# Indexed attention of the first block: index dots ahead of the query products, VectorE's list in a new order, a later fourth query product, an earlier start of the output product

## The reference, cut to what matters

```
q, c, qi, ki, wi = split(h @ w_in)            # 1024, 128, 8x64, 64, 8 columns
c = rms_norm(c, kv_norm_g)
dots  = relu(einsum('bqhd,bsd->bqhs', qi, ki))            # 8 index heads
score = einsum('bqh,bqhs->bqs', wi, dots), causal
idx   = top_k(score, 64)                                  # per query
logits = (q @ w_uk * scale) . c[idx] + rel_bias, causal   # 16 heads
o = softmax(logits) . c[idx] @ w_uv
x = x + o @ w_o ;  x = x + relu(norm(x) @ w_up)**2 @ w_down
```

## Time and profile before

| | us |
|---|---|
| median of 3 runs (range) | 885.27 (882.36 to 885.95) |
| the profiled execution: its time | 883.13 |
| its span | 881.0 |
| TensorE busy | 858.1 (97%) |
| VectorE busy | 686.0 (78%) |
| ScalarE busy | 474.8 (54%) |
| GpSimd busy | 137.3 (16%) |

### The profile page before, as it was taken

How to read it: one execution, slowest core, us unless ns; L and a number is a source line. 1 busy time by engine, 2 the same in 40 slices (tenths; PEclk the granted TensorE clock), 3 DMA queues, 4 the chain that set the end, 5 groups by cost and what they waited for, 6 DMA issues and landing times.

```text
span 881.0 us, 17947 instructions
## 1 busy us (share of the span) xinstructions
PE 858.1 (97%) x7016; PEld 818.4 (93%) x7016; DVE 686.0 (78%) x1074; ACT 474.8 (54%) x698; POOL 137.3 (16%) x154
## 2 busy tenths in 40 slices
PE   6999999999999987899999999999999999999998
PEld 5998999999999985599999999999889999999998
DVE  4897789898876698667666677678658998997884
ACT  7783365555444346656655444354357647645742
POOL 6230100014311000000000122232204213013000
PEclk9999999999999997999999999999999999999999
DMA  9755767779998432046655666656536554454652
GB/s 348 256 209 188 269 219 250 241 241 281 264 256 214 151 108 84 2 144 197 206 192 194 196 197 196 195 190 191 178 130 194 150 176 155 145 190 147 198 185 96
DMA packets 46960, 167.86 MB, mean 191 GB/s; under 512 B 5776, under 2 KB 5920, under 8 KB 46640
## 3 DMA queue, kind: packets, MB, share of 16 engines
q1 hardware_dynamic: 40896, 146.82, 50.6%
q0 software_dynamic: 5856, 20.00, 8.3%
q10 hardware_dynamic: 144, 0.15, 0.1%
HBM read 165.50 MB, written 1.44 MB: 189 GB/s over the span
## 4 chain that ended last, share of the span: by engine, by line
PE 90%; DVE 6%; ACT 2%; issue 1%; DMA 1%; POOL 0%; DVEq 0%; SPq 0%; ACTq 0%
PE bank L551 25%; PE bank L547 25%; PE bank L552 25%; PE bank L618 5%; PE bank L636 2%; PE bank L781 1%; DVE wlo L1329 1%; PE bank L876 1%; PE bank L886 1%; PE bank L835 1%; PE bank L837 1%; PE bank L836 1%; DVE score L1631 1%; DVE lt L1680 1%; DMA plain<-plain_w 1%
## 5 line engine op out<-in xcount | busy, mean ns | idle before, releaser
L1329 DVE TENSOR_TENSOR wlo<-raw,whi 128x1024 fp32r<-128x1024 f32 x260 | 320.5, 1265 | 91.7 <-ACT whi L971 91.4
L551 PE MATMUL bank<-xl,whi 128*128 128x256 f32 x1328 | 369.6, 278 | 0.0
L552 PE MATMUL bank<-xh,wlo 128*128 128x256 f32 x1328 | 368.4, 277 | 0.0
L547 PE MATMUL bank<-xh,whi 128*128 128x256 f32 x1310 | 367.4, 280 | 0.2 <-DVE wlo L1329 0.2
L971 ACT ACTIVATE whi<-raw 128x1024 fp32r<-128x1024 f32 x260 | 265.6, 1053 | 144.7 <-PE bank L552 129.3
L547 PEld LDWEIGHTS bank<-xh,whi 128*128 128x128 f32 x1310 | 245.8, 188 | 9.2 <-issue 7.4
L551 PEld LDWEIGHTS bank<-xl,whi 128*128 128x128 f32 x1328 | 249.4, 188 | 0.3
L552 PEld LDWEIGHTS bank<-xh,wlo 128*128 128x128 f32 x1328 | 249.3, 188 | 0.0
L551 PE MATMUL bank<-hlo,whi 128*128 128x256 f32 x512 | 141.8, 277 | 0.0
L552 PE MATMUL bank<-hhi,wlo 128*128 128x256 f32 x512 | 141.4, 276 | 0.0
L547 PE MATMUL bank<-hhi,whi 128*128 128x256 f32 x506 | 139.9, 276 | 0.0
(11 more groups left out here) (290 smaller groups left out, 1089.1 us busy)
## 6 DMA issues: line engine op xcount, KB each, us to landing
raw<-weights SPq DMA_DIRECT2D x260, 512.0 KB, 4.4
ada_raw<-ada_w POOLq DMA_DIRECT2D x24, 512.0 KB, 4.7
plain<-plain_w SPq DMA_DIRECT2D x16, 512.0 KB, 6.7
relB<-rel_scratch POOLq DMA_DIRECT2D x8, 256.0 KB, 7.7
bl<-rpb_in POOLq DMA_DIRECT2D x32, 64.0 KB, 3.6
x<-x_in SPq DMA_DIRECT2D x4, 256.0 KB, 6.2
cond<-cond_in POOLq DMA_DIRECT2D x1, 1024.0 KB, 7.8
cx<-ctx_in POOLq DMA_DIRECT2D x1, 1024.0 KB, 7.2
```

The lines of the kernel that those rows point to most:

```text
L547: mmul(dst, hi, rh, start=start, stop=False)
L551: mmul(dst, hi, rlo, start=False, stop=False)
L552: return mmul(dst, lo, rh, start=False, stop=stop)
L1329: V_.tensor_tensor(wlo[:, sl], raw[:, sl], whi[:, sl].bitcast(F32), ALU.subtract)\
```

## The change

The unit `q` of four becomes three units and, behind `ukuv` in the order of the weights, one unit `q_last`. On TensorE the sum of squares of c moves into the third `lat` unit, dots 0 to 3 stand ahead of the first query unit and dots 4 to 7 ahead of the second, in four banks (2 to 5) with four `rl` buffers. The fourth query unit's two chunks stand around `logits(2)`, in bank 1. The first chunk of `att_out` stands in pieces between the last groups, each tile of depth behind a wait for its group; the second follows the last group. `outs` uses bank 0 in place of 1. On VectorE the norm of c goes ahead, all first-block scores come together, and the second block's top-k is done before the fourth group's logits are read. The split of `att_out`'s first unit moves into the rounds of the groups, in halves. ScalarE runs a one-column Exp ahead of the K copies.

```
-          ("lat", 3), ("q", 4), ("ukuv", 1), ("att_out", 4), ...
+          ("lat", 3), ("q", 3), ("ukuv", 1), ("q_last", 1), ("att_out", 4), ...
-            rl = sb("rl", [P, 2, 512], F32, room)
+            rl = sb("rl", [P, 4, 512], F32, room)
+        DOTS = (bank[4], bank[5], bank[2], bank[3])
-        OUTS = (bank[7], bank[1])
+        OUTS = (bank[7], bank[0])
...
# TensorE
-            stage("lat", xs, skip=1)
+            stage("lat", xs, skip=1, n=1)
+            gemm(U0["lat"] + 2, 1, F0["lat"] + 2, xs, ahead_of=latent_square_sum)
...
             pe.wait_ge(S_["bank_emptied"], F0["lat"] + 3)
-            for j in range(4):
-                dots(2 * j)
...
-                dots(2 * j + 1)
-                stage("q", xs, skip=j, n=1)
+            dots(0)
+            dots(1)
...
+            dots(2)
+            dots(3)
+            stage("q", xs, n=1)
+            for g in range(4, 8):
+                dots(g)
+            stage("q", xs, skip=1)
...
             for g in range(NG + 3):
                 if g == 1:
                     pe.wait_ge(S_["kv_emptied"], 8)
+                if g == 2:
+                    q_last(0)
+                if g == 3:
+                    pe.wait_ge(S_["bank_emptied"], F0["q"] + 4)
                 if g < NG:
                     logits(g)
+                if g == 2:
+                    q_last(1)
+                if g == NG + 1:
+                    att_out_first(0, 0, 5)
                 if 2 <= g < NG + 2:
                     turn(pt, 3, "probs_ready", "turned_copied", "probs_turned", g - 2)
+                if g == NG + 2:
+                    att_out_first(0, 5, 6)
                 if g >= 3:
                     outs(g - 3)
-            pe.wait_ge(S_["outs_lo"], NG)
-            stage("att_out", hcs)
+            att_out_first(0, 6, DT)
+            att_out_first(1, 0, DT)
+            stage("att_out", hcs, skip=1)
...
# ScalarE
+            ahead(U0["q"] + 2)
             ahead(U0["ukuv"])
+            A(den[:, 0, 0:1], eps[:], ACT.Exp)
...
             for g in range(NG + 3):
+                if g == 8:
+                    half(U0["att_out"], 0)
+                if g == NG + 1:
+                    half(U0["att_out"], 1)
                 if g < NG:
                     softmax(g)
...
# VectorE
+            for g in range(4):
+                scores(g)
+            ahead(U0["q"])
+            topk(0, 0, 2)
+            queries(0)
...
+            topk(0, 2, 4)
+            ahead(U0["q"] + 1)
+            topk(0, 4, 8)
+            queries(1)
+            ahead(U0["q"] + 2)
+            scores(4)
+            scores(5)
+            queries(2)
+            scores(6)
+            scores(7)
             ahead(U0["ukuv"])
-            topk(1, 0, 4)
+            topk(1, 0, 2)
...
-                if g < 4:
-                    topk(1, 4 + g, 5 + g)
+                if g == 0:
+                    topk(1, 2, 3)
+                if g == 1:
+                    topk(1, 3, 5)
+                if g == 2:
+                    topk(1, 5, 6)
+                    queries(3)
+                    topk(1, 6, 8)
+                if g == 9:
+                    half(U0["att_out"], 0)
+                if g == NG + 2:
+                    half(U0["att_out"], 1)
```

More of the change, by code:

```diff
@@ L46 @@
 STAGES = [("xr", 2), ("gate", 4), ("up0", 16), ("down0", 16),
[1 row of a table removed]
+          ("lat", 3), ("q", 3), ("ukuv", 1), ("q_last", 1), ("att_out", 4), ("up1", 16), ("down1", 16),
           ("ck", 2), ("cv", 2), ("k", 2), ("q2", 2), ("v", 2), ("ca", 2), ("cg", 2), ("za", 2), ("cz", 2),
@@ L575, in unit @@
                                 first_wait(k)
+                            if ahead_of is not None and c == 0:
+                                ahead_of(k)
                             mm = acc3(b[:, c * S:(c + 1) * S], (2 * r + c) % 4, k * P, *rhs(k), k == 0, k == DT - 1,
@@ L718, in _ @@
             pe.wait_ge(S_["bank_emptied"], F0["lat"] + 3)
-            for j in range(4):
-                dots(2 * j)
[L721 to L729, removed]
-                dots(2 * j + 1)
-                stage("q", xs, skip=j, n=1)
+            dots(0)
+            dots(1)
+            pe.wait_ge(S_["wi_rows"], 1)
+            pe.wait_ge(S_["consts_loaded"], 16)
+            for b in range(QB):
+                for i in range(2):
+                    mm = mmul(OUTB[:, S + b * H_IDX:S + (b + 1) * H_IDX], wit[:, b * P:(b + 1) * P],
+                              ident[0:2 * H_IDX, i * H_IDX:(i + 1) * H_IDX], start=i == 0, stop=i == 1)
+            mm.then_inc(S_["wi_cols"], 1)
+            dots(2)
[4 more added lines that the diff above has]
+            stage("q", xs, skip=1)
             u = U0["ukuv"]
             pe.wait_ge(S_["c_lo"], 1)
+            pe.wait_ge(S_["dots_relu"], 8)
             chunk_ready(0, 0, 2 * u)
@@ L737, in _ @@
                 if n == 4:
-                    pe.wait_ge(S_["bank_emptied"], F0["q"] + 4)
+                    pe.wait_ge(S_["bank_emptied"], F0["q"] + 3)
                 j = 2 * KV_BANK[n // 2] + n % 2
@@ L799, in _, with q_last, att_out_first @@
             pe.wait_ge(S_["c_root"], 1)
+            def q_last(c):
+                u = 2 * U0["q_last"] + c
+                chunk_ready(0, 0, u)
+                for k in range(DT):
+                    mm = acc3(bank[1][:, c * S:(c + 1) * S], u % 4, k * P, *xs(k), k == 0, k == DT - 1)
+                mm.then_inc(S_["chunk_used"], 1)
+            def att_out_first(c, k0, k1):
+                u = 2 * U0["att_out"] + c
+                if k0 == 0:
+                    chunk_ready(0, 0, u)
+                for k in range(k0, k1):
+                    pe.wait_ge(S_["outs_lo"], 4 + k + 1)
+                    mm = acc3(bank[1][:, c * S:(c + 1) * S], u % 4, k * P, *hcs(k), k == 0, k == DT - 1)
+                if k1 == DT:
+                    mm.then_inc(S_["chunk_used"], 1)
             for g in range(NG + 3):
@@ L984, in ahead, with half @@
                 next_split(u // 4, u % 4)
+            def half(u, c):
+                split_chunk(u // 4, 2 * (u % 4) + c)
             def x_hi(t, g):
@@ L1652, in _, with queries @@
             dve.wait_ge(S_["caus_loaded"], 16)
[L1653 to L1666, removed]
+            def queries(j):
+                full(U0["q"] + j if j < 3 else U0["q_last"])
+                b = bank[(F0["q"] + j) % 2] if j < 3 else bank[1]
+                emptied(V_.scalar_tensor_tensor(qT[:, 2 * j:2 * j + 2], two(b), ATT_SCALE, wide(R[:, 0]), ALU.mult, ALU.mult))
+            for g in range(4):
+                scores(g)
+            ahead(U0["q"])
+            topk(0, 0, 2)
+            queries(0)
+            dve.wait_ge(S_["c_hi"], 1)
+            V_.tensor_tensor(cnl[:], cn[:], cnh[:].bitcast(F32), ALU.subtract).then_inc(S_["c_lo"], 1)
+            topk(0, 2, 4)
+            ahead(U0["q"] + 1)
+            topk(0, 4, 8)
[6 more added lines that the diff above has]
+            scores(7)
             ahead(U0["ukuv"])
-            topk(1, 0, 4)
+            topk(1, 0, 2)
             def read_logits(g):
@@ L2015, in lay_weights @@
     g["lat"] = tiles(np.concatenate([wa[:, qe:qie], wa[:, qie:kie], wa[:, qie:kie]], 1))
-    g["q"] = tiles(wa[:, :qe])
+    q = tiles(wa[:, :qe])
+    g["q"], g["q_last"] = q[:3], q[3:]
     g["ukuv"] = np.concatenate([i["att_w_uk"][0].transpose(2, 0, 1).reshape(P, D),
```

42 lines of the change are left out of this document (21 added, 21 removed), and 1 row of the table STAGES.

## The result

The changed kernel takes 874.91 us (median of 4 runs, 874.13 to 875.46); the kernel before, on the same chip, 883.82 (4 runs, 881.99 to 885.95). The ratio is 0.9895, interval 0.9879 to 0.9912: 8.9 us less.

A forecast was written before the change was run, and what follows sets the result against it. TensorE's idle time was taken as the shadow of VectorE's list up to the second mask. The second `att_out` chunk comes 9.1 us earlier: 883.1 - 9.1 = 874.0, or 876.2 as median; middle 875.0, range 871 to 878.6.

The forecast's parts named there:

- VectorE's list: VectorE from the copy of `wi` to the second mask: 48.66 us less 10.05 leaves 38.6, plus 0.3 charged for margin.
- The norm of c: On VectorE, moved to where it waited for the third `lat` unit: saves 2.2 us, cost taken as 0, at most 0.5.
- TensorE keeps up: TensorE up to the fourth query unit: ends at 334.0, VectorE wants it at 334.2, margin 0.2 us, 0.3 charged.
- Rival B: TensorE's list is the later one: K and V copies and load take 2 to 3 us more; 877.5 us, chance 0.12.
- The table load: On ScalarE ahead of the K copies: adds 1.3 us by the trace, without the extra drain the Trainium skill counts.
- Mask to `read_logits(4)`: On VectorE, `read_logits(3)` and `norm_probs(2)` stand between second mask and `read_logits(4)`: 1.85 us, so that read at 339.6.
- Now the clock should be full: Round from `read_logits(4)` to the next: full clock but group 3's softmax inside, so kept at 3.3 us, giving 342.9.
- rival A: Clock falls once after TensorE idles 2.1 us behind `logits(4)`; four rounds at half clock cost 3.4: 878.4 us, chance 0.19.
- The tail: Last read to second `att_out` chunk: +1.6 for matmuls ahead of `turn(11)`, +0.9 last split, -2.1 fewer tiles, sum +0.4 us.
- Everything behind runs as before: After the second `att_out` chunk: nothing changes, and feeding the raw slots one chunk later costs nothing.
- Rival C: The gain does not show: half clock, late TensorE list and a 2.2 us split price together; 882.6 us, chance 0.04.
- D: Slower: half clock from the V copies to the output product costs 13.0 us; 888.0 us, chance 0.03.

The follow-up runs named there:

- e7_dots_back: Changed kernel with dots 2 and 3 put back behind the first query unit: 879.57 us, ratio 0.9945 to the kernel before.
- e5_copies_first: Changed kernel with ScalarE, from group 3 on, copying older groups' transposes and outputs ahead of the new group's softmax: 869.95 us, ratio 0.9844 to the kernel before.
- e6_no_exp_ahead: Changed kernel without the one-column Exp ahead of the K copies, so the table load returns to the first softmax: 874.63 us.

## Why the prediction was right or wrong

The time, 874.91 against 875.0, came out closer than its steps did, and that was luck. By steps, in the profiled execution:

- *VectorE's list, 38.6 and 0.3 of margin:* right. It is 38.65, and the repeat has 38.65. The terms of VectorE's list were never measured one by one. What was undone singly are TensorE's two moves that feed it: putting the dots back brings a wait of 5.25, and the fourth unit 3.96. The norm of c cost nothing that shows in its new place: `wi` starts at 299.34 and, in the repeat, at 298.57, against 298.82 before. But by `e7_dots_back` its 2.2 hangs on the early dots, which I had listed as terms of their own.
- *TensorE keeps up, with 0.2 to spare, "the tightest place":* right in kind, too tight in size. The unit ends at 333.9 as counted, though all started 0.5 later than in the sum. VectorE comes for it at 334.68, so the margin is 0.8 and nothing was charged for it. Rival B did not happen. With the unit ahead of the K product the list loses 4.06; so 48 matmuls in gaps "without cost to the end" was the right reading, and with the dots the largest part of the change.
- *The table load:* the row decided rightly. The next instruction started 1.30 us after the load did, as before with 1.34, and taking the Exp away moves the time by nothing that shows. The 1.3 us that the Trainium skill's count (ScalarE: Activation LUTs, "What ACT_TABLE_LOAD costs") would have added are not there.
- *Mask to `read_logits(4)`, 1.85:* right, 339.75 - 337.99 = 1.76.
- *"Now the clock should be full ... I keep 3.3":* wrong, and the step that failed. `read_logits(5)` came 4.69 us after `read_logits(4)`, and the rounds to the last took 20.89 where I had 3.3 + 14.6 + 0.4 = 18.3. This is rival A, to which I gave 0.19; it happened in both profiles of the changed kernel, and the mean clock of all its eight runs, 0.996 to 0.998, is below the 0.999 to 1.000 of the filled version. The gap I had worked out as 2.1 is 1.90. With the gap filled the same stretch takes 18.30, what the forecast said, so its sum holds for a full clock and lacks the fall. Its parts hold less well: the first round is 3.72 there and not 3.3, and the six behind it take 14.58, as the 14.57 before, so the split had no price. A's price of 3.4 was too high: the fall costs 2.6 in this execution and 1.5 in the repeat. The clock is back within two rounds, or one, and not four; but the second round at half clock took 3.98 where the filled one took 2.24, twice the 0.84 that I had charged.
- *The tail, +0.4:* too high. From the last read to the second chunk it is 369.86 - 360.64 = 9.22. Before, it was 376.99 - 367.45 = 9.54; the forecast had worked it out as 9.46. So the change is -0.3. That the early product "buys nothing" is right, and shown: 9.26 without it. What I overcharged is the last split. With the split in place and the product late the tail is still 0.3 shorter than before; its 1.22 us on VectorE leave TensorE a wait of 0.36 for the last `hcl`, and before that wait was 0.70. The row from which the tail before is read:

```profile
376.99 0.28 PE L547 MATMUL bank<-hch,whi 128*128 128x256 f32 x1
```

- *Everything behind runs as before:* nearly. From the second chunk to the end of the execution it is 875.46 - 369.86 = 505.60, against 883.13 - 376.99 = 506.14. The 0.5 are not the change's; see the last section.

The sum again: against my 367.8 the second chunk is late by 0.5 (the start) - 0.2 (list and margin) - 0.1 (mask to read) + 2.6 (rounds) - 0.6 (tail) = 2.1 with roundings. Less 0.6 (the 0.5 behind it, and 0.1 by which I had the second chunk before too early), the profiled execution is 1.5 over my 874.0: its gain is 7.7 us and not 9.1. The median is right to 0.1 because I had added 1.0 for the place of the profiled execution among its runs, and the profiled execution after happens to be the slowest of its four. Taken as mechanism, the likeliest case was wrong: what ran was the forecast's list together with A's clock, at 44 to 76% of A's price.

Rival C needed three losses, and had one. D needed half clock for the whole stretch; it held for 6.8 us.

Two rows of the kernel before would have told more, and the prediction's reading left them out. TensorE's waits are not all the shadow of VectorE's list: the second longest, 2.47 us ahead of `turn(1)`, is for ScalarE's copy. And the gap of 1.68 did not leave the clock alone. TensorE works again from 340.26, and the stretch from 340 to 342 us has 0.90 already, which is half clock in its last 0.4 us, before the gap of 2.47 begins at 341.86. So a gap shorter than the one that A foresaw had been followed by the fall, and A deserved more than 0.19.

```profile
340.00:342.00 2.00, 1.61 (x14) 1.21 (x14) 1.93 (x14) 0.89 (x6) 0.00 (x0) 0.90 0.00 0
```

```profile
344.33 1.09 PE L781 MATMUL bank<-ident,pt 128*128 128x128 f32 x4 [2.47 <-ACT pT L1177]
```

What the forecast did not see at all is in `e5_copies_first`. The rows had it: ScalarE's copy is the releaser of a turn here and in the earlier trace rows, and I took the round of 2.43 as given where 2.24 was to be had.

## What to carry to other kernels

When one engine's ordered list sets the end, add up its rows from a fixed start to the point that others wait for, and price a reordering by the waits that it removes; that sum, 38.6 us, was right to 0.05 us here. Then look at the first gap which the new order opens on TensorE: a gap of 1.90 us between short groups of matmuls was followed by half clock in all four profiles that have it, and its cost is in the rounds behind it. In the kernel with ScalarE's copies first, where the longest gap there was 0.90, the clock stayed up. On an engine that serves two partners, put the short copy that another engine waits for ahead of the long work whose input has only just been asked for: 5.0 us here, more than either moved part of TensorE's program brought.

## What the runs showed of the hardware

TensorE's step between matmuls of 256 columns has two values at the granted clock 1.00, and both occur in every execution. In the first profile of the changed kernel, 42 matmuls of the first query unit take 305.29 - 300.35 = 4.94 us, 117.6 ns each:

```profile
300.35 0.28 PE L548 MATMUL bank<-xh,whi 128*128 128x256 f32 x1
...
305.29 0.28 PE L548 MATMUL bank<-xh,whi 128*128 128x256 f32 x1
```

In the same profile the 24 matmuls of `att_out`'s second chunk take from the 369.86 shown above to the start of the next chunk, 2.72 us or 113.3 ns each:

```profile
372.58 0.28 PE L548 MATMUL bank<-hch,whi 128*128 128x256 f32 x1
```

In the repeat, the same kernel takes 370.85 - 368.02 = 2.83 us for as many, 117.9 ns each:

```profile
368.02 0.28 PE L548 MATMUL bank<-hch,whi 128*128 128x256 f32 x1
...
370.85 0.28 PE L548 MATMUL bank<-hch,whi 128*128 128x256 f32 x1
```

Mostly the place in the program goes with the value: in all eleven profiles the mean step is 113.3 ns from 116 to 229 us and 117.7 or 117.8 in the first query unit. `att_out` is a place where executions differ. Its last seven chunks have the shorter step in two of the eleven profiles, this one and `e6_no_exp_ahead`, and the longer one in nine. The 0.11 us a chunk make up to 0.8 us over the seven; the 0.5 that the profiled execution gained behind the second chunk lies within that. The attention's start, too, shifts between profiles by up to 1.4 us (298.57 to 299.98), and by 0.77 between the two of the changed kernel. I did not find what decides either. It is the reason for measuring from a fixed instruction here and not from the span's start.
